# Six of eight output tiles of each down projection by one level of Strassen's scheme, with both MLPs split in two K parts

## The chip, the cores and the metric

The kernel runs on one core of a Trainium2 chip. The metric is the device time of one execution in microseconds (us). TensorE (PE) does the matmuls, ScalarE (ACT), VectorE (DVE) and GpSimd (POOL) the rest, SyncE (SP) starts the DMAs.

## The reference, cut to what matters

Three transformer layers run one after the other on 512 tokens of width 1024 (the first has 16 meta tokens besides). All is float32. The parts that the change touches are the three feed-forward blocks:

```python
def swiglu(h, w_gate, w_up, w_down):                 # first block, D_FF = 2816
    return (jax.nn.silu(h @ w_gate) * (h @ w_up)) @ w_down

def sq_relu_mlp(x, w1, w2):                          # layers 0 and 1 of the second block, D_FF_2 = 4096
    h = jax.nn.relu(x @ w1)
    return (h * h) @ w2
...
        h = rms_norm_2(x, norm_mlp_pre[layer])
        x = x + rms_norm_2(sq_relu_mlp(h, mlp_w1[layer], mlp_w2[layer]), norm_mlp_post[layer])
```

## The kernel before

Activations lie transposed: features on the 128 partitions, tokens along the columns. A projection is a set of output tiles (128 output features x 512 tokens) and each tile sums K blocks of 128 input features in one PSUM bank. Float32 accuracy comes from three fp16 matmuls for each block: high weight times high activation, high times low, low times high (L975 to L977 in `tile_T`).

**The weight stream.** All weights come as one stream of 128x128 blocks, 8 blocks (512 KB) to a unit, 317 units. SP loads each unit into `w_raw`, a ring of 6 units (`RAW`). ScalarE makes `w_hi` (fp16, scaled by `WS`) in `split_hi`, L1476; VectorE makes `w_lo`, the rest, in `split_lo`, L1878; both go into rings of 8 units (`WR`). SP loads a new unit when `lo_split` says that its place was split. ScalarE waits with `mm_done` for the matmuls that used the place it overwrites. TensorE waits for `lo_split` at a new unit.

**What sets the order.** Each engine runs a queue written out in advance; semaphores count. The class `Plan` walks over the table `STAGES` (name, kind, tiles, K, width) and numbers blocks, units, PSUM evictions (`evicted`) and banks: successive tiles take banks 0, 1, 2, 3 of `pS` in turn, in some stages also `pT` and `pO` (six in turn, `SIX`). `out_of(s, n)` on ScalarE and VectorE first runs the splits up to six units ahead, then waits until tile n's last matmul is done. So each of these two engines alternates between weight splits and evictions.

**The stages of the change.** `ffgu` (44 tiles, gate and up of the first block, K = 8 blocks) is followed by `ffd` (8 tiles, K = 22); `up0` (32 tiles, K = 8) by `dn0` (8 tiles, K = 32), and the same for `up1` and `dn1`. The first four tiles of an up stage (`lead`) are made together, block by block, while the norm before them is still arriving. VectorE evicts an up tile, squares it, ScalarE writes the high half into `ffh` and VectorE the low half.

**The end of a down projection.** For seven tiles VectorE copies the bank out (`taken`, L2517; in `ffd` it adds to X), ScalarE squares the result, and VectorE adds the squares up in `acc`. The eighth tile is computed in two token halves of 256 columns (`out_halves`, L998 to L1000, all K blocks for the first 256 tokens, then all for the others). While TensorE makes the second half, the first half's sum of squares goes through a matmul with ones (L990, L992, ahead of the second half's step 8), ScalarE takes Ln and Exp (L1536, L1538), and VectorE runs the first half of the post-norm over eight tiles (L2540, L2544). After the second half comes the same for the other tokens: the square (L1545), the eviction (L2549), the sum (L1012), Ln and Exp (L1547, L1549), and the second loop (L2561, L2567), which in layer 0 also writes the next norm's input tile by tile (L1485, L1893). The sums of squares of the two MLPs carry the names `mb` and `md`. Small matmuls on constant data (`unread`, L1130) stand between.

Of the kernel before, what the change touches and what calls it, by code (L numbers as in the profile page):

```python
# [35 lines left out]
P = 128  # L36
T = 512
# [20 lines left out]
UW = TPU * P  # L58
RAW = 6
WR = 8  # L60
# [7 lines left out]
LEADS = ("qa", "ffgu", "cv", "up0", "kvc", "up1")  # L68
SIX = ("ffgu", "cv", "up0", "up1")
SPARE = ("ks", "qb")  # L70
HOME = {"ck2": 4, "cv2": 5}
INSIDE = {"va": 0, "vb": NQ, "vm": 0, "vv": 0}


class Stage:


    def __init__(self, name, kind, n, k, width, o0, tau0):
        self.name, self.kind, self.n, self.k, self.width, self.o0, self.tau0 = name, kind, n, k, width, o0, tau0

    def tile(self, j, k):
        if self.name in LEADS and j < LEAD:
            return self.tau0 + k * LEAD + j
        return self.tau0 + (j * self.k + k if self.kind == "T" else k * self.width)


class Plan:
# [6 lines left out]
    def __init__(self):  # L94
        self.st, self.order = {}, []
        self.o = self.tau = self.ms = 0
        self.out_ms, self.unit_ms, self.out_tau, self.marks = [], {}, [], set()
        for name, kind, n, k, width in STAGES:
            while kind == "N" and self.tau % width:
                self.tau += 1  # L100
                if self.tau % TPU == 0:
                    self.unit_ms[self.tau // TPU - 1] = self.ms
# [3 lines left out]
            if kind == "T":  # L106
                if name in LEADS:
                    for kk in range(k):
                        for j in range(LEAD):
                            self.step(self.tau, 1, kk == k - 1)  # L110
                for j in range(LEAD if name in LEADS else 0, n):
                    for kk in range(k):
                        self.step(self.tau, 1, kk == k - 1)
            else:
                for t in range(n):
                    for kk in range(k):
                        tau = self.tau + kk * width
                        last = kk == k - 1
                        ends = t == n - 1 and (tau + width) % TPU == 0
# [6 lines left out]
                        if ends:  # L126
                            self.unit_ms[tau // TPU] = self.ms
                self.tau += k * width
                self.o += n
        self.n_units = -(-self.tau // TPU)  # L130
        self.bank, self.before = [], []
        turn, last = 0, {}
        for s in self.order:
            for j in range(s.n):
# [32 lines left out]
    def step(self, tau, width, last):  # L167
        ends = (tau + width) % TPU == 0
# [7 lines left out]
        if ends:  # L176
            self.unit_ms[tau // TPU] = self.ms
        self.tau += width
# [7 lines left out]
    + [("wo", "T", KD, KD, 1), ("ffgu", "T", 2 * KFF1, KD, 1), ("ffd", "T", KD, KFF1, 1),  # L186
       ("cv", "T", 12, KD, 1), ("ckv", "T", 2, KD, 1), ("kr", "T", 1, KD, 1), ("cq", "T", 6, KD, 1),
       ("kn", "T", 4, 2, 1), ("qr", "T", 2, 6, 1), ("qn", "T", 4, 6, 1), ("vm", "N", NQ, 2, 4),
       ("awo", "T", KD, KD, 1), ("up0", "T", KFF2, KD, 1), ("dn0", "T", KD, KFF2, 1),
# [3 lines left out]
       ("cwo", "T", KD, KD, 1), ("up1", "T", KFF2, KD, 1), ("dn1", "T", KD, KFF2, 1)]  # L193
# [6 lines left out]
SRC = [("mrg", 8), ("ff", KFF1), ("xb", 8), ("conv", 4), ("p1", 8), ("h0", KFF2), ("p2", 8), ("hid", 2),  # L200
       ("p3", 8), ("h1", KFF2), ("out", 16)]
# [28 lines left out]
def whole_units(name):  # L230
    return -(-PL.st[name].tau0 // TPU) * TPU
# [303 lines left out]
def splits(s, j):  # L535

    return 1 if s.name in LEADS and j < LEAD else s.k // TPU + 1
# [4 lines left out]
def build_program(nc, x_in, stream, consts, params, aux, out):  # L542
    ctx = ExitStack()
    with ctx:
# [6 lines left out]

        w_raw = sb("w_raw", [P, RAW, UW])
        w_hi = sb("w_hi", [P, WR, UW], F16)
        w_lo = sb("w_lo", [P, WR, UW], F16)
# [47 lines left out]
        ARENA = 20864  # L602
# [44 lines left out]
        ffh, at = pair(0, [KFF2, T])  # L647
        stage_c, _ = view(ARENA - KEEP_TO, [KEEP_TO])

# [25 lines left out]
        z, _ = pair(at, [5, T])  # L675
# [88 lines left out]
        raw_loaded = [sem(f"raw_loaded{i}") for i in range(RAW)]  # L764
# [67 lines left out]
        half_taken = sem("half_taken")  # L832
        lse_ln = sem("lse_ln")
# [45 lines left out]
        def m_view(m, n):  # L879

            return m_att[:, n, :] if m == "mc" else xx32[:, n, 0:T]

# [4 lines left out]
        def _(pool):  # L887
# [9 lines left out]
            norm_power("x0", meta=True)  # L897
            filled = [0]
# [21 lines left out]
            pool.wait_ge(mm_done, PL.out_ms[S["ffd"].o0 + KD - 1])  # L920
# [7 lines left out]
            pool.wait_ge(mm_done, PL.out_ms[S["dn0"].o0 + KD - 1])  # L928
# [4 lines left out]
            norm_power("p2")  # L933


        @block.tensor
        def _(pe):
            unit = [-1]

            def weights(tau, n=1):  # L940

                u = tau // TPU
# [5 lines left out]
                a = (tau % TPU) * P  # L948
                return w_hi[:, u % WR, a:a + n * P], w_lo[:, u % WR, a:a + n * P]
# [31 lines left out]
            def out_halves(s, m, rhs):  # L981

                n, q, o = HALVED.index(m), PL.q[m] + KD - 1, s.o0 + KD - 1
                bank_free(o)
                for half, ps in enumerate((pT[:, 0, 0:HT], out_bank(o)[:, HT:T])):
                    a = slice(half * HT, half * HT + HT)
                    for k in range(s.k):
# [7 lines left out]
                        tau = s.tile(KD - 1, k)  # L995
# [20 lines left out]
            def out_last(s, m, rhs):  # L1016
# [4 lines left out]
                else:  # L1021
                    out_T(s, KD - 1, rhs, inside=lambda: early_sum(m))
                    direct_norm(m)

# [330 lines left out]
            for j in range(KD - 1):  # L1355
                out_T(S["ffd"], j, of(ffh), rhs_wait=None if j else PL.r["ff"])
            out_last(S["ffd"], "x2", of(ffh))
# [101 lines left out]
        def _(act):  # L1459
# [1403 lines left out]
```

## Time and profile before

| | us |
|---|---|
| median of 3 runs | 2057.53 (2056.46 to 2060.12) |
| profiled execution, its own span | 2056.2 |
| TensorE busy | 1992.2 (97%) |
| VectorE busy | 1188.0 (58%) |
| ScalarE busy | 825.8 (40%) |
| GpSimd busy | 31.3 (2%) |

The span runs from the first to the last instruction of the profiled execution; the runs' times are 1 us longer in the median. A matmul's row shows its start and a modelled duration, and matmuls overlap, so what one costs is read from the distance between starts.

### The profile page before, as it was taken

What the parts mean: (1) busy time and instruction counts of PE and PEld (TensorE: products, weight loads), DVE (VectorE), ACT (ScalarE), POOL (GpSimd) and SP (SyncE); (2) the same over time, 40 slices, a digit from 0 to 9 for tenths busy, and PEclk for the clock granted to TensorE, in tenths of its full rate; (3) what the DMA queues carried; (4) which work ended last, traced back from release to release, by engine and by line L of the source; (5) the groups of instructions that cost most, each with busy time, mean ns of one, the idle gap of its engine ahead of it and who ended that gap; (6) DMA issues with size and microseconds to landing.
All of it is one profiled execution on the core that took longest, in us unless ns stands there. A gap on an engine that the chain in (4) does not pass through costs nothing. (4 is left out here: it accounts for less than half of the span.)

```text
span 2056.2 us, 27740 instructions
## 1 busy us (share of the span) xinstructions
PE 1992.2 (97%) x10751; PEld 965.9 (47%) x10756; DVE 1188.0 (58%) x2199; ACT 825.8 (40%) x1507; POOL 31.3 (2%) x36
## 2 busy tenths in 40 slices
PE   9989999999999999999999999999989999999998
PEld 4444444444444454444444444555544444444445
DVE  6979744546554347676575632259866636765223
ACT  4447733323333233346443322236377744432220
POOL 2000000000000002000000000000000000000000
PEclk9999999999999999999999999999999999999999
DMA  6300233324333222312233333217200031433311
GB/s 220 101 1 1 73 103 103 95 72 131 103 103 112 93 91 93 104 52 73 72 113 105 102 111 103 82 42 226 85 1 1 23 101 44 142 102 105 111 52 41
DMA packets 54345, 179.19 MB, mean 87 GB/s; under 512 B 6224, under 2 KB 11984, under 8 KB 53968
## 3 DMA queue, kind: packets, MB, share of 16 engines
q1 hardware_dynamic: 54224, 177.51, 28.0%
q8 instruction: 85, 1.39, 0.3%
q14 instruction: 36, 0.29, 0.0%
HBM read 174.34 MB, written 2.10 MB: 86 GB/s over the span
## 5 line engine op out<-in xcount | busy, mean ns | idle before, releaser
L1878 DVE SCALAR_TENSOR_TENSOR w_lo<-w_raw,w_hi 128x1024 f16<-128x1024 f32 (+1 forms) x317 | 384.4, 1217 | 178.2 <-ACT w_hi L1476 143.4
L1476 ACT ACTIVATE w_hi<-w_raw 128x1024 f16<-128x1024 f32 x316 | 330.0, 1048 | 247.8 <-PE pS L977 234.4
L975 PE MATMUL pS<-xx,w_hi 128*128 128x512 f16 x920 | 349.3, 380 | 2.4 <-DVE xx L1893 1.4
L977 PE MATMUL pS<-xx,w_lo 128*128 128x512 f16 x920 | 349.4, 380 | 0.0
L976 PE MATMUL pS<-xx,w_hi 128*128 128x512 f16 x920 | 349.2, 380 | 0.0
L975 PE MATMUL pS<-arena,w_hi 128*128 128x512 f16 x824 | 312.3, 379 | 1.4 <-DVE arena L1893 1.4
L976 PE MATMUL pS<-arena,w_hi 128*128 128x512 f16 x824 | 312.3, 379 | 0.0
L977 PE MATMUL pS<-arena,w_lo 128*128 128x512 f16 x824 | 312.3, 379 | 0.0
L1485 ACT ACTIVATE arena<-src 128x512 f16<-128x512 f32 x107 | 69.2, 647 | 322.0 <-DVE src L2581 166.7
L977 PEld LDWEIGHTS pS<-xx,w_lo 128*128 128x128 f16 x920 | 90.0, 98 | 109.0 <-issue 0.8
L975 PEld LDWEIGHTS pS<-xx,w_hi 128*128 128x128 f16 x920 | 90.2, 98 | 107.9 <-DVE xx L1893 2.2
L976 PEld LDWEIGHTS pS<-xx,w_hi 128*128 128x128 f16 x920 | 90.1, 98 | 104.0 <-issue 1.5
L975 PEld LDWEIGHTS pS<-arena,w_hi 128*128 128x128 f16 x824 | 80.7, 98 | 99.2 <-DVE arena L1893 1.9
L976 PEld LDWEIGHTS pS<-arena,w_hi 128*128 128x128 f16 x824 | 80.7, 98 | 97.5 <-issue 0.7
L977 PEld LDWEIGHTS pS<-arena,w_lo 128*128 128x128 f16 x824 | 80.7, 98 | 97.3
L1209 PE MATMUL pS<-arena 128*128 128x512 f16 (+3 forms) x480 | 103.0, 315 | 1.5 <-DVE arena L2159 1.5
L2093 DVE TENSOR_REDUCE st_max<-pT 128x1 f32<-128x512 f32 (+3 forms) x140 | 68.1, 507 | 39.3 <-PE pT L1182 32.0
L1589 ACT ACTIVATE tmp<-pS 128x512 f32<-128x512 f32 (+2 forms) x152 | 80.2, 538 | 24.5 <-PE pS L1217 16.2
L1893 DVE SCALAR_TENSOR_TENSOR arena<-src,arena 128x512 f16<-128x512 f32 x107 | 74.8, 699 | 24.9 <-ACT arena L1485 24.7
L2517 DVE TENSOR_SCALAR xx<-pS 128x512 f32<-128x512 f32 x21 | 14.5, 692 | 124.6 <-PE pS L977 124.6
L1572 ACT ACTIVATE pT<-pT,st_max 128x512 f32<-128x512 f32 (+3 forms) x140 | 72.5, 518 | 33.7 <-DVE st_max L2093 32.4
L1947 DVE TENSOR_TENSOR tmp<-pS,rs 128x512 f32<-128x512 f32 x46 | 31.7, 690 | 83.4 <-PE pS L977 83.4
(393 smaller groups left out, 2918.0 us busy)
## 6 DMA issues: line engine op xcount, KB each, us to landing
w_raw<-in_w SPq DMA_DIRECT2D x317, 512.0 KB, 3.6
X<-in_x SPq DMA_DIRECT2D x8, 264.0 KB, 6.9
arena<-in_c SPq DMA_DIRECT2D x2, 1024.0 KB, 6.1
out_t<-X SPq DMA_DIRECT2D x16, 128.0 KB, 1.7
arena<-in_h SPq DMA_DIRECT2D x4, 256.0 KB, 12.7
arena<-in_h SPq DMA_DIRECT2D x2, 512.0 KB, 9.7
arena<-in_c SPq DMA_DIRECT2D x2, 256.0 KB, 2.9
arena<-arena SPq DMA_DIRECT2D x4, 128.0 KB, 2.5
```

The source lines that it names most:

```text
L975: pe.matmul(ps, wh, ah, start=f, stop=False)
L976: pe.matmul(ps, wh, al, start=False, stop=False)
L977: mm = pe.matmul(ps, wl, ah, start=False, stop=l)
L1209: pe.matmul(ps[:, c0:c0 + n], k[:, ks_], q[:, qs], start=x == 0, stop=False)
L1476: act.activation(w_hi[:, u % WR, :], w_raw[:, u % RAW, :], ACT.Copy, scale=WS).then_inc(hi_split, 1)
L1485: act.activation(dst, a, ACT.Identity, scale=scale).then_inc(rhs_hi, 1)
L1572: ins = act.activation(a, a, ACT.Exp, bias=stat(st_max, t)[:, x:x + 1], accum_out=stat(st_sum, t)[:, x:x + 1])
L1589: act.activation(exps(u)[:, 0:a.shape[1]], a, ACT.Exp).then_inc(key_exped, 1)
L1878: dve.scalar_tensor_tensor(out=w_lo[:, u % WR, a:UW], in0=w_raw[:, u % RAW, a:UW], scalar=WS, in1=w_hi[:, u % WR, a:UW], op0=ALU.mult, op1 ...
L1893: dve.scalar_tensor_tensor(out=dst, in0=a, scalar=scale, in1=h, op0=ALU.mult, op1=ALU.subtract).then_inc(rhs_ready, 1)
L1947: dve.tensor_tensor(dst, ps, r[:, 0:T], ALU.mult).then_inc(evicted, 1)
L2093: ins = dve.tensor_reduce(stat(st_max, t)[:, x:x + 1], nat_bank(c)[:, c0:c0 + n], AX.X, ALU.max, negate=True)
```

## The change

**Strassen groups.** In each down projection tiles 1 to 6 become three groups. A group takes two output tiles, the two token halves of 256 columns, and the K blocks in pairs (even and odd), as a 2x2 by 2x2 product of blocks. Seven products replace eight: each has K/2 steps of three matmuls with 256 columns. The seven stationary operands are A11, A22 and A12 themselves and the sums S2, S3, S1, S4; the moving ones are B blocks and the combinations T1 to T4 of activations. A12 accumulates onto A11's bank, after ScalarE has copied that bank (`first_copy`, L1744). Tile 0 and tile 7 stay plain; tile 0's steps wait for the activations pair by pair (`out_pair`).

**Weight sums.** GpSimd makes four sums a group in `w_raw`, in place (`add_weights`): A21 += A11 (that is S3), then A22 becomes S2 = S3 + A22 (after A22 was split), A11 becomes S1 = S2 - A11, A12 becomes S4 = S2 + A12 (after A12 was split). There are 60 of them, 128x1024 or, in the first block, 128x1408 elements. ScalarE's splits of the sums wait for `summed`.

**K parts.** Each MLP runs as `up0a` (16 tiles), `dn0a` (all 8 output tiles, K = 16), `up0b` (16 tiles), `dn0b` (K = 16, VectorE adds to the stored result). `ffd` keeps K = 22. The two halves at the end of `dn0b` and `dn1b` have K = 16; there ScalarE's squares now wait for VectorE's evictions.

**Rings.** The three weight rings hold 66 blocks each, with units of 8, or of 11 in the first block's groups; ten load semaphores; SP's loads are written out without a loop. VectorE's and ScalarE's splits of 128x1024 become 360 in place of 318 (some are wider); hidden activations are written in pairs of tiles, with the token combinations made by VectorE (`mix_tokens`, three operations a pair).

The core of the diff:

```diff
-    + [("wo", "T", KD, KD, 1), ("ffgu", "T", 2 * KFF1, KD, 1), ("ffd", "T", KD, KFF1, 1),
+    + [("wo", "T", KD, KD, 1), ("ffgu", "T", 2 * KFF1, KD, 1), ("ffd0", "T", 1, KFF1, 1), ("ffds", "S", 3, KFF1 // 2, 1), ("ffd7", "T", 1, KFF1, 1),
...
-       ("awo", "T", KD, KD, 1), ("up0", "T", KFF2, KD, 1), ("dn0", "T", KD, KFF2, 1),
+       ("awo", "T", KD, KD, 1), ("up0a", "T", UP_A, KD, 1)] + down(0, "a") + [("up0b", "T", KFF2 - UP_A, KD, 1)] + down(0, "b")
...
+PRODUCTS = (("A11", 0, B11), ("A22", 4, T4), ("A12", 0, B21), ("S2", 1, T2), ("S3", 2, T3), ("S1", 3, T1), ("S4", 5, B22))
...
+def down(lay, part):
+
+    k = UP_A if part == "a" else KFF2 - UP_A
+    return [(f"dn{lay}{part}0", "T", 1, k, 1), (f"dn{lay}{part}s", "S", 3, k // 2, 1), (f"dn{lay}{part}7", "T", 1, k, 1)]
...
+                for g in range(s.n):
+                    s.banks.append([last.get(b, -1) for b in range(6)])
+                    o = s.o0 + N_READ * g
+                    last.update({0: o, 1: o + 1, 4: o + 2, 3: o + 3, 2: o + 4, 5: o + 5})
...
+                    pool.tensor_tensor(w["A21"], w["A11"], w["A21"], ALU.add).then_inc(summed, 1)
+                    pool.wait_ge(summed, first + 1)
+                    pool.wait_ge(lo_split, units_["A22"] + 1)
+                    pool.tensor_tensor(w["A22"], w["A21"], w["A22"], ALU.add).then_inc(summed, 1)
+                    pool.wait_ge(summed, first + 2)
+                    pool.tensor_tensor(w["A11"], w["A22"], w["A11"], ALU.subtract).then_inc(summed, 1)
+                    pool.wait_ge(lo_split, units_["A12"] + 1)
+                    pool.tensor_tensor(w["A12"], w["A22"], w["A12"], ALU.add).then_inc(summed, 1)
...
+            def strassen(s, g, ops, copies):
+
+                free = s.banks[g]
+                for x, (name, b, op) in enumerate(PRODUCTS):
+                    if name == "A12":
+                        pe.wait_ge(first_copied, copies + g + 1)
+                    elif free[b] >= 0:
+                        pe.wait_ge(evicted, free[b] + 1)
...
+                    for k in range(s.k):
+                        tau = s.factor(g, x, k)
+                        wh, wl = weights(tau)
+                        oh, ol = ops[0][:, k, a], ops[1][:, k, a]
+                        pe.matmul(ps, wh, oh, start=k == 0 and name != "A12", stop=False, skip_group_check=True)
...
+            def first_copy(s, g, copies, f):
+
+                ms, tau = s.first_ms[g]
+                split_hi(tau, look=0)
+                act.wait_ge(evicted, s.o0 + (N_READ * (g - 1) + 2 if g else 0))
+                act.wait_ge(mm_done, ms)
+                act.activation(x1c, pS[:, 0, 0:HT], ACT.Copy, scale=f).then_inc(first_copied, 1)
...
+            def mix_tokens():
...
+                link(dve.tensor_tensor(in_two(sums[:, 0:T]), in_two(b[:, HT:3 * HT]), twice(b[:, 3 * HT:4 * HT]), ALU.subtract))
...
-                if m == "x2":
+                if m in ("x2", "mb", "md"):
                     act.wait_ge(evicted, o + 1)
...
             sp.wait_ge(mm_done, PL.out_ms[S["kvc"].o0 - 1])
+            sp.wait_ge(rhs_ready, PL.r["p2"] + KD)
```

VectorE's queue at the start of layer 0's down projection stood like this before (`xx` holds the result, `acc` the squares):

```order
L1878 SCALAR_TENSOR_TENSOR w_lo<-w_raw,w_hi 128x1024 [waits hi_split] x4
L2517 TENSOR_SCALAR xx<-pS 128x512 [waits mm_done]
L1900 COPY acc<-sq 128x512 [waits squared]
L1878 SCALAR_TENSOR_TENSOR w_lo<-w_raw,w_hi 128x1024 [waits hi_split] x4
L2517 TENSOR_SCALAR xx<-pS 128x512 [waits mm_done]
L1903 TENSOR_TENSOR acc<-acc,sq 128x512 [waits sq_summed,squared]
```

Now, at the start of part a, tile 0 and the first group stand there like this (`arena` holds the result, `tmp` the intermediate combinations):

```order
L2753 TENSOR_SCALAR arena<-pS 128x512 [waits mm_done]
L2180 SCALAR_TENSOR_TENSOR w_lo<-w_raw,w_hi 128x1024 [waits hi_split] x2
L2753 TENSOR_SCALAR arena<-pS 128x256 [waits mm_done]
L2180 SCALAR_TENSOR_TENSOR w_lo<-w_raw,w_hi 128x1024 [waits hi_split] x2
L2764 SCALAR_TENSOR_TENSOR tmp<-pS,tmp 128x256 [waits first_copied,mm_done]
L2766 SCALAR_TENSOR_TENSOR tmp<-pT,tmp 128x256 [waits evicted]
L2180 SCALAR_TENSOR_TENSOR w_lo<-w_raw,w_hi 128x1024 [waits hi_split] x2
L2768 SCALAR_TENSOR_TENSOR tmp<-pS,tmp 128x256 [waits mm_done]
L2774 SCALAR_TENSOR_TENSOR arena<-pS,tmp 128x512 [waits evicted]
L2180 SCALAR_TENSOR_TENSOR w_lo<-w_raw,w_hi 128x1024 [waits hi_split]
L2780 SCALAR_TENSOR_TENSOR arena<-pO,tmp 128x256 [waits mm_done]
```

One eviction for every four splits has become six evictions for every seven splits.

ScalarE's queue in the same place, before (high halves of units, and the squares of evicted tiles):

```order
L1476 ACTIVATE w_hi<-w_raw 128x1024 [waits mm_done,raw_loaded0]
L1497 ACTIVATE sq<-xx 128x512 [waits sq_summed,evicted]
L1476 ACTIVATE w_hi<-w_raw 128x1024 [waits mm_done,raw_loaded1]
L1476 ACTIVATE w_hi<-w_raw 128x1024 [waits mm_done,raw_loaded2]
L1476 ACTIVATE w_hi<-w_raw 128x1024 [waits mm_done,raw_loaded3]
```

Now, from the copy of one group's first product to that of the next:

```order
L1744 ACTIVATE tmp<-pS 128x256 [waits mm_done,evicted]
L1735 ACTIVATE w_hi<-w_raw 128x1024 [waits raw_loaded2,mm_done]
L1735 ACTIVATE w_hi<-w_raw 128x1024 [waits raw_loaded1,mm_done]
L1735 ACTIVATE w_hi<-w_raw 128x1024 [waits raw_loaded3,mm_done]
L1735 ACTIVATE w_hi<-w_raw 128x1024 [waits summed,mm_done] x4
L1744 ACTIVATE tmp<-pS 128x256 [waits mm_done,evicted]
```

Four splits a group wait for GpSimd's sums, and they stand ahead of the next copy.

VectorE's queue at the end of layer 0's last down projection, from the end of the first half's loop to the second loop, before:

```order
L2544 TENSOR_TENSOR X<-X,tmp 128x256 [waits dve_chain] x2
L1878 SCALAR_TENSOR_TENSOR w_lo<-w_raw,w_hi 128x1024 [waits hi_split] x4
L2549 TENSOR_SCALAR xx<-pS 128x256 [waits squared,mm_done]
L2561 SCALAR_TENSOR_TENSOR tmp<-xx,par,rs 128x256 [waits dve_chain,rs_direct,half_taken]
L2567 TENSOR_TENSOR X<-X,tmp 128x256 [waits dve_chain]
```

And now:

```order
L2921 TENSOR_TENSOR X<-X,tmp 128x256 [waits dve_chain] x2
L2180 SCALAR_TENSOR_TENSOR w_lo<-w_raw,w_hi 128x1024 [waits hi_split] x2
L2752 SCALAR_TENSOR_TENSOR arena<-pS,arena 128x256 [waits mm_done]
L2936 SCALAR_TENSOR_TENSOR tmp<-arena,par,rs 128x256 [waits dve_chain,rs_direct,half_taken]
L2942 TENSOR_TENSOR X<-X,tmp 128x256 [waits dve_chain]
```

Two splits have left this place, and the eviction no longer waits for ScalarE's square.

## Rows read from the trace of the kernel before

**Rows 1.** The head of the page, busy time, share of the span, instructions.

```profile
span 2056.2 us, 27740 instructions
PE 1992.2 (97%) x10751; PEld 965.9 (47%) x10756; DVE 1188.0 (58%) x2199; ACT 825.8 (40%) x1507; POOL 31.3 (2%) x36
```

**Rows 2.** Table by stretches: length, busy time by engine, PEclk, DMA share, GB/s.

```profile
667.00:753.60 86.60, 86.60 (x436) 42.48 (x434) 26.01 (x28) 20.57 (x22) 0.00 (x0) 1.00 0.27 84
...
1183.00:1338.00 155.00, 155.00 (x768) 74.88 (x767) 46.24 (x50) 35.16 (x37) 0.00 (x0) 1.00 0.31 97
...
1355.10:1359.10 4.00, 3.99 (x11) 1.49 (x12) 3.21 (x7) 2.73 (x5) 0.00 (x0) 0.57 0.62 239
```

**Rows 3.** Lines by form, 1183 to 1338: busy, mean ns | idle before, releaser.

```profile
L1878 DVE SCALAR_TENSOR_TENSOR w_lo<-w_raw,w_hi 128x1024 f16<-128x1024 f32 x28 | 34.2, 1223 | 61.6 <-ACT w_hi L1476 61.6
L1903 DVE TENSOR_TENSOR acc<-acc,sq 128x512 f32<-128x512 f32 x6 | 4.1, 683 | 0.1
...
L1476 ACT ACTIVATE w_hi<-w_raw 128x1024 f16<-128x1024 f32 x28 | 29.6, 1056 | 92.7 <-PE pS L977 92.7
```

**Rows 4.** Timeline, TensorE in `ffd`: start, duration, instruction.

```profile
739.82 0.38 PE L975 MATMUL pS<-arena,w_hi 128*128 128x512 f16 x1
...
746.08 0.38 PE L977 MATMUL pS<-arena,w_lo 128*128 128x512 f16 x1
746.29 0.27 PE L998 MATMUL pT<-arena,w_hi 128*128 128x256 f16 x1
...
751.32 0.27 PE L999 MATMUL pT<-arena,w_hi 128*128 128x256 f16 x1
```

**Rows 5.** Timeline at the end of tile 6 of `dn1`.

```profile
2022.23 0.38 PE L977 MATMUL pS<-arena,w_lo 128*128 128x512 f16 x1
...
2022.45 0.27 PE L998 MATMUL pT<-arena,w_hi 128*128 128x256 f16 x1
...
2022.65 0.69 DVE L2517 TENSOR_SCALAR xx<-pS 128x512 f32<-128x512 f32 x1 [17.16 <-PE pS L977]
...
2023.26 0.68 DVE L1903 TENSOR_TENSOR acc<-acc,sq 128x512 f32<-128x512 f32 x1
```

**Rows 6.** Timeline of the tail of `dn1`, from the second half on.

```profile
2032.93 0.27 PE L998 MATMUL pS<-arena,w_hi 128*128 128x256 f16 x1
...
2037.58 0.88 DVE L2540 SCALAR_TENSOR_TENSOR tmp<-xx,par,rs 128x256 f32<-128x256 f32 x2 [3.54 <-ACT rs L1538]
...
2042.76 0.76 DVE L2544 TENSOR_TENSOR X<-X,tmp 128x256 f32<-128x256 f32 x2
...
2044.91 0.38 ACT L1545 ACTIVATE sq<-pS 128x256 f32<-128x256 f32 x1 [7.37 <-PE pS L1000]
2046.08 0.47 ACT L1547 ACTIVATE rs<-pO,eps 128x256 f32<-128x256 f32 x1 [0.79 <-PE pO L1012]
2046.59 0.42 ACT L1549 ACTIVATE rs<-rs 128x256 f32<-128x256 f32 x1
...
2047.10 0.48 DVE L2561 SCALAR_TENSOR_TENSOR tmp<-xx,par,rs 128x256 f32<-128x256 f32 x1 [1.27 <-ACT rs L1549]
```

**Rows 7.** Timeline of the tail of `dn0`.

```profile
1337.99 0.27 PE L998 MATMUL pS<-arena,w_hi 128*128 128x256 f16 x1
...
1348.49 4.62 DVE L1878 SCALAR_TENSOR_TENSOR w_lo<-w_raw,w_hi 128x1024 f16<-128x1024 f32 x4
1353.04 0.41 DVE L2549 TENSOR_SCALAR xx<-pS 128x256 f32<-128x256 f32 x1
1353.37 0.47 DVE L2561 SCALAR_TENSOR_TENSOR tmp<-xx,par,rs 128x256 f32<-128x256 f32 x1
...
1355.11 0.40 PE L1081 MATMUL pS<-xx,w_hi 128*128 128x512 f16 x1 [2.06 <-ACT xx L1485]
```

**Rows 8.** GpSimd's lines by form: busy, mean ns of one.

```profile
L895 POOL TENSOR_TENSOR rt<-rt,half_neg 128x4 f32<-128x4 f32 x4 | 4.1, 1014 | 469.0 <-DVE rt L1912 469.0
...
L902 POOL MEMSET arena<- 128x768 f32 x1 | 0.7, 738 | 0.1
...
L902 POOL MEMSET arena<- 128x512 f32 x1 | 0.5, 526 | 0.1
```

More of the change, by code:

```diff
@@ L105, in __init__ @@
             self.order.append(s)
-            if kind == "T":
+            if kind == "S":
+                for g in range(n):
+                    self.group(s, g)
+            elif kind == "T":
                 if name in LEADS:
@@ L118, in __init__ @@
                         last = kk == k - 1
-                        ends = t == n - 1 and (tau + width) % TPU == 0
+                        ends = t == n - 1 and full[kk]
                         if last or ends:
@@ L165, in __init__, with tile, group, step @@
             at += n
-    def step(self, tau, width, last):
-        ends = (tau + width) % TPU == 0
+    def tile(self):
+        if not self.open:
+            self.raw.append(len(self.raw_size))
+            self.freed.append(len(self.size))
+            self.size.append(0)
+            self.raw_size.append(0)
+            self.open = True
+        self.unit.append(len(self.size) - 1)
+        self.off.append(self.size[-1])
+        self.size[-1] += 1
+        self.raw_size[-1] += 1
+        self.open = self.size[-1] < TPU
+    def group(self, s, g):
+        raw = {name: len(self.raw_size) + n for n, name in enumerate(RAWS)}
+        v = {name: len(self.size) + n for n, (name, _, _) in enumerate(PRODUCTS)}
+        self.raw_size += [s.k] * len(RAWS)
+        self.freed += [v[FREED_BY[name]] for name in RAWS]
+        self.sums[v["S2"]] = (raw, v, self.n_sums)
+        self.n_sums += 4
+        ends = []
+        for name, _, _ in PRODUCTS:
+            self.size.append(s.k)
+            self.raw.append(raw[HELD_IN[name]])
+            self.unit += [v[name]] * s.k
+            self.off += range(s.k)
+            self.tau += s.k
+            self.ms += 1
+            self.marks.add((self.tau - 1, 0))
+            self.unit_ms[v[name]] = self.ms
+            ends.append((self.ms, self.tau - 1))
+        s.first_ms.append(ends[0])
+        for x in (2, 3, 3, 5, 5, 6):
+            self.out_ms.append(ends[x][0])
+            self.out_tau.append(ends[x][1])
+        self.o += N_READ
+    def step(self, tau, last):
+        self.tile()
+        ends = not self.open
         if last or ends:
@@ L176, in step, with reach @@
         if ends:
-            self.unit_ms[tau // TPU] = self.ms
-        self.tau += width
+            self.unit_ms[self.unit[tau]] = self.ms
+        self.tau += 1
+    def reach(self, tau, look, stop):
+        now = self.unit[tau]
+        v = now + 1
+        while v < min(now + 1 + look, stop) and self.after[v] <= now - 2:
+            v += 1
+        return v
+def down(lay, part):
+    k = UP_A if part == "a" else KFF2 - UP_A
+    return [(f"dn{lay}{part}0", "T", 1, k, 1), (f"dn{lay}{part}s", "S", 3, k // 2, 1), (f"dn{lay}{part}7", "T", 1, k, 1)]
 STAGES = (
@@ L230, in whole_units, with unit_at, raw_at @@
 def whole_units(name):
-    return -(-PL.st[name].tau0 // TPU) * TPU
+    t = PL.st[name].tau0
+    return PL.unit[t] + (PL.off[t] > 0)
+def unit_at(name):
+    return PL.unit[PL.st[name].tau0]
+def raw_at(name):
+    return PL.raw[unit_at(name)]
 CAUSAL_NAT = (((3, 0, 0, 4 * P),), ((2, 0, 0, 3 * P), (0, 3 * P, 0, P)), ((1, 0, 0, 2 * P),))
```

578 lines of the change are left out of this document (407 added, 171 removed).

## The prediction

> **What bounds the kernel now.** I read the head of the page first: TensorE is busy 1992.2 of 2056.2 us, VectorE 58% of it [rows 1]. That is an average, so I took the table by stretches next: in the plain run of the down projections TensorE has no gap at all (86.60 of 86.60 us in the first block's, 155.00 of 155.00 in layer 0's), while VectorE works 26.01 and 46.24 us there [rows 2]. The same stretch's list of lines says what VectorE does: 28 splits of a weight unit into its low half at 1.223 us, whose idle time is ended by ScalarE's high half [rows 3], and that one waits for TensorE to give back ring places. So in these stages a matmul removed is time removed, provided the other engines follow. Around them are places where TensorE does wait: the tails of the down projections, where a norm runs (term 3).
>
> The profiled execution spans 2056.2 us; the median of the runs is 2057.53. I make the sum on the span and add 1.3.
>
> **Term 1, the matmuls.** Over one step of K a tile costs three matmuls of 512 columns. Between the starts at 739.82 and 746.08 lie 29 of them: 0.2159 us each. Half-width ones run from 746.29 to 751.32 in 46 steps: 0.1093 us each, so the weight load does not show at 256 columns either [rows 4]. A group of two plain tiles costs 2K x 3 x 0.2159 = 1.295K; as Strassen products it is 7 x K/2 x 3 x 0.1093 = 1.148K. Three groups save 0.443K. K is 22 in the first block and 32 in each MLP (two parts of 16): 0.443 x 86 = 38.1 us off. The other tiles and the up projections keep their matmuls.
>
> **Term 2, banks handed over at once.** Before, consecutive tiles lie in different banks, so an eviction costs TensorE nothing. Now tile 0 of each MLP part, the first product after it, tile 7 of part a and the first tile of the second up half all use bank 0 of pS. At three places a layer (tile 0 to A11 in both parts, tile 7 to the up half) TensorE must wait for the eviction of what it has just finished. The end of a tile of before prices it: the last matmul starts at 2022.23, the next could at 2022.45; VectorE starts its eviction at 2022.65, takes 0.69, and its next operation starts at 2023.26 [rows 5]. TensorE would go on at about 2023.3, 0.85 us late. Six places cost 5.1 us. In layer 0's part b VectorE lays a bias first and has splits ahead of that eviction: up to 0.9 more. I take 6.0 (bounds 3, were banks handed over at the operation's first columns, and 10, were a 1.2 us split ahead at half the places and more).
>
> **Term 3, the tails of the two MLPs.** Before, the last tile's second half holds 32 steps, 32 x 3 x 0.1093 = 10.5 us, and beside it the first half's norm runs on VectorE. Now it holds 16, 5.25 us; term 1 counted this as if the end came 5.25 us earlier, since the rest of part b's K was moved ahead of the second up half. But the norm's loop is as long as before. In layer 1 the second half starts at 2032.93, VectorE's loop runs from 2037.58 to 2043.52 (t+4.65 to t+10.6), the square follows at 2044.91 and the second loop begins at 2047.10, t+14.2 [rows 6]. After: the sums of the norm stand at the same step (k = 8), so the loop ends at t+10.6 again. Then come the eviction (0.47), ScalarE's square, which now waits for that eviction (0.4), the matmul with ones (0.7), Ln and Exp (0.9): with hand-overs the second loop begins at about t+13.3. It gains 0.9 of the 5.2, so 4.3 us are lost. In layer 0 the loop ends at t+10.5 (1348.49 less 1337.99), four splits ran before the eviction, and the second loop began at t+15.4 [rows 7]. Now two splits stand there (2.4 us): eviction at 12.9, square, sum, Ln, Exp: t+15.5. Nothing is gained and 5.3 lost. TensorE is then idle some 6 to 7 us in each tail; after a 2.06 us wait before 1355.11 the stretch behind it shows a granted clock of 0.57 [rows 2, 7], so the small matmuls after the longer gap may run at the lower level: 1 us. Term 3 is +10.6 (9 to 13).
>
> **Term 4, do the other engines follow?** A group's seven products last 7 x 24 x 0.1093 = 18.4 us in an MLP part and 25.2 in the first block. VectorE does seven splits (8.5 us at 1.22; in the first block 1408 columns wide, about 1.6 each by the step from 512 to 1024 columns) and six evictions of some 3 us: 11.5 in part a, 14 in part b with the additions to the old value and the squares, 16.7 in the first block. ScalarE: seven halves at 1.05, a copy, two squares, 9 us. Both fit.
>
> GpSimd is the unknown: 60 additions of two weight blocks, no such row in the trace. From below: VectorE handles 1024 columns of two operands in 1.22 us. From above: a GpSimd memset of 512 columns takes 526 ns, of 768 738, about 1 ns a column with one access each [rows 8]; three accesses of 1.03 would be 3.2 us. In between, the fixed part of its 128x4 operation (1.014) plus one pass over 1024 columns is 2.1; I take it, as the trace's only two-input GpSimd operation shows that start. Four sums are then 8.4 us of 18.4, 9.8 of 25.2 in the first block. *The Trainium skill, "GPSIMD Engine Reference", section 3.1, gives 4497 ns for an add of 2048 columns; halved, an estimate of 2.25 us a sum, it would move the total by under 1 us. No trace row bears on it.*
>
> Latency: ScalarE's split of a sum waits for GpSimd, and behind it in ScalarE's queue stands the copy of the next group's first product, for which the third product waits. In an MLP part the unit rings let the sums run about half a group ahead; in the first block, where a block takes 11 of the ring's 66 places, raw loads wait for splits of the group in flight and I find 2 us of room (a group's raw blocks are 44 of 66, so half the next group's loads wait for this group's splits of S3 and S4). I put +4 for this, nearest to the case of sums at 2.1 us (0 with sums at VectorE's price; the upper end is rival B).
>
> The up halves: a pair of tiles lasts 48 x 0.2159 = 10.4 us; VectorE does two evictions, the token sums, two wide low halves and two splits, 1.4 + 1.5 + 2.4 + 2.4 = 7.7. The last pair is ready some 5.7 us after tile 0 begins, and tile 0 takes it last. Cost nothing while VectorE keeps 2 us of room a pair. On SP an added wait for the second norm of layer 1 stands ahead of the compressed bias; behind it are queued the weight loads from the stage q2b on, which the ring would not take earlier anyway, since 16 units of other stages lie before them: nothing.
>
> **Sum:** 2056.2 - 38.1 + 6.0 + 10.6 + 4 = 2038.7 span, 2040 us.
>
> **Rivals.**
>
> A, the smaller losses: the sums never show and hand-overs cost 3: 2056.2 - 38.1 + 3 + 9 + 1.3 = 2031. For it: VectorE and ScalarE have 40% of a group free.
>
> B, **slower**: VectorE and GpSimd do not run side by side. Place: the groups. If VectorE's operations on two SBUF operands (splits, additions, squares) and GpSimd's sums take turns, a group needs at 3.2 us a sum 8.5 + 12.8 = 21.3 us in part a, 11 + 12.8 = 23.8 in part b (2.5 more for the additions and two squares at 0.683 [rows 3]) and 13.7 + 17.6 = 31.3 in the first block: 2.9 x 6 + 5.4 x 6 + 6.1 x 3 = 68 us over TensorE's time. Tiles 0 give each of five stages some 8 us of lead, 40 in all at best, so 28 to 68: with 45 in place of the 4 the time is 2081. It decides from 26 us in all, 1.7 a group, with the lead a sum of 2.6 to 3. Against it: no row shows VectorE slowed beside GpSimd, which works only 31.3 us in all [rows 1], nearly all of it memsets. *The Trainium skill, "SBUF — State Buffer", section "SBUF: two separate sides", states this: a VectorE instruction with two SBUF inputs and a GpSimd instruction that reads SBUF hold a shared port pair in turn, whichever starts first. No row here shows it or denies it.*
>
> C, turns at the middle price: at 2.4 us a sum, part b lacks 11 + 9.6 - 18.4 = 2.2 a group and VectorE's blocked queue delays evictions too; about +17 instead of +4: 2053.
>
> D, the change does less than it says: the products at 256 columns cost more than 0.1093, because their stationary blocks change at every matmul. There are 3 x 43 x 21 = 2709 of them; at 0.114 they give back 12.7 us: 2053. Against it, the 46 even steps in rows 4, with a new weight load each.
>
> **How the numbers follow.** Forecast 0.50 (2034 to 2050), A 0.15, B 0.15, C 0.15, D 0.05. About 0.2% (4 us) is what a measurement here can tell from no change. Forecast and A are faster; C and D straddle 2053.4, half each: faster 0.75, same 0.09, slower 0.16. The range reaches from 2030 to 2062 and leaves out most of B and a little of A.
>
> **What would show it.** TensorE's start-to-start in the products at 0.109; gaps of some 0.85 us at the first product of each part and at the first tile of the second up half; second norm loops starting t+13.3 and t+15.5; GpSimd's sums near 2.1 us; the wait before the third product (A12) on ScalarE's copy under 1 us. Wrong would be: sums of 3 us, or VectorE's splits stretched well over 1.22 us beside them, or waits of TensorE for low splits inside the groups.

## The result, and the profile after

The changed kernel takes 2096.52 us (2092.26 to 2097.2), the one before 2057.21 in the same comparison: a ratio of 1.0187 (95% interval 1.0174 to 1.0200). It is slower; the forecast was 2040, with 2062 as the upper end. The profiled execution spans 2090.4 us; it was the fastest of the four, 4.3 us under the median. The head of its page answers to [rows 1]:

```profile
span 2090.4 us, 29726 instructions
PE 1970.2 (94%) x11816; PEld 1074.7 (51%) x11821; DVE 1435.5 (69%) x2400; ACT 949.0 (45%) x1628; POOL 212.0 (10%) x96
```

TensorE's busy time fell by 22 us, yet it now waits 120 us instead of 64. Which waits these are, the list of TensorE's waits says (line waited for, then us in total, times, longest):

```profile
PE pS L1239 <- ACT tmp L1744: 18.6, 6, 6.1
PE pO L1212 <- ACT sq L1835: 13.2, 3, 6.3
PE pS L1239 <- issue: 11.3, 4, 5.1
...
PE pS L1331 <- DVE w_lo L2180: 6.7, 1, 6.7
PE pS L1269 <- DVE arena L2195: 6.5, 4, 3.3
...
PE pS L1173 <- DVE arena L2753: 1.6, 2, 0.8
```

L1239 is the first matmul line of a Strassen product, L1744 ScalarE's copy of a group's first product, L1269 tile 0 of a part. The third line ("issue": nothing that the profile shows released it) is the first product of each MLP part, which waits for tile 0's bank. L1173 is here the first tile of the second up half, which waits for tile 7's bank. L1212 stands in the tails. The wait at L1331 lies at the very start of the program, where the change was not expected to do anything.

The table by stretches answers to [rows 2]: the groups of the first block, of part b in layer 0 and in layer 1, then the wait for one first copy and what follows it (length, busy by engine, granted clock, DMA share, GB/s):

```profile
670.58:758.95 88.37, 79.44 (x694) 69.42 (x693) 63.76 (x48) 30.17 (x29) 30.38 (x9) 0.94 0.33 117
1299.50:1362.91 63.41, 58.58 (x504) 50.79 (x505) 43.62 (x47) 24.98 (x29) 20.98 (x7) 0.94 0.40 140
2000.66:2062.39 61.73, 56.92 (x504) 49.88 (x505) 40.06 (x43) 19.81 (x24) 20.99 (x7) 0.97 0.15 51
705.60:709.20 3.60, 0.00 (x0) 0.00 (x0) 3.60 (x2) 1.27 (x4) 2.36 (x1) 0.57 0.00 0
709.20:712.80 3.60, 3.56 (x17) 2.55 (x18) 2.20 (x2) 2.51 (x2) 0.00 (x0) 0.50 0.52 153
```

Three groups should last 75.7 us in the first block and 55.0 in a part; they take 88.4, 63.4 and 61.7. After this wait TensorE restarts at a granted clock of 0.50, the lower of its two levels, 1.2 GHz: 17 matmuls in 3.6 us where 33 fit.

From the starts of the products and tiles in the trace the whole difference comes together (us; a gain is negative):

| place | forecast | measured |
|---|---|---|
| matmuls of the products | -38.1 | -38.1 (2.62 and 3.60 us a product) |
| start of the program | 0 | +9.8 |
| tile 0 of the four MLP parts, until the first product | +4.3 | +20.8 |
| tile 7 of part a to the up half | +1.7 | +1.9 |
| waits for the first copy, six | +4 | +19.6 |
| lower clock level inside the groups | 0 | +11.4 |
| tails of the three down projections | +10.6 | +12.8 |
| other stages, between the blocks | 0 | -4.0 |
| span | -17.5 | +34.2 |

Tile 0, for instance, starts at 1115.84 and the first product at 1132.44: 16.6 us where 48 matmuls of 0.2159 last 10.4.

```profile
1115.84 0.38 PE L1269 MATMUL pS<-arena,w_hi 128*128 128x512 f16 x1
...
1132.44 0.37 PE L1239 MATMUL pS<-arena,w_hi 128*128 128x256 f16 x1 [2.19 <-issue]
```

The place of the last row is the attention of layer 1, and the row belongs to this one execution, not to the change. From its first plain tile (1406.74) to that of the next up half (1757.43) it takes 350.7 us here, 354.0 in the kernel before, and 354.8 in the run with the start mended, whose code in that place is the changed kernel's. In the middle of it (1485 to 1600) the granted clock is 0.99 here and 0.96 in that run.

**What VectorE does beside a sum.** The trace's timeline in the first block, GpSimd and VectorE together (start, duration):

```profile
693.92 0.41 DVE L2768 SCALAR_TENSOR_TENSOR tmp<-pS,tmp 128x256 f32<-128x256 f32 x1
694.14 3.16 POOL L1085 TENSOR_TENSOR w_raw<-w_raw 128x1408 f32<-128x1408 f32 x1 [3.16 <-DVE w_lo L2180]
694.37 3.48 DVE L2771 TENSOR_TENSOR X<-X,tmp 128x512 f32<-128x512 f32 x1
697.38 3.50 POOL L1087 TENSOR_TENSOR w_raw<-w_raw 128x1408 f32<-128x1408 f32 x1
697.77 3.39 DVE L2772 TENSOR_TENSOR X<-X,tmp 128x256 f32<-128x256 f32 x1
701.19 0.69 DVE L2774 SCALAR_TENSOR_TENSOR X<-pS,X 128x512 f32<-128x512 f32 x1
...
703.50 4.47 POOL L1089 TENSOR_TENSOR w_raw<-w_raw 128x1408 f32<-128x1408 f32 x1 [2.62 <-DVE w_lo L2180]
...
704.87 0.41 DVE L2752 SCALAR_TENSOR_TENSOR X<-pO,X 128x256 f32<-128x256 f32 x1
705.20 3.04 DVE L2202 COPY acc<-sq 128x512 f32<-128x512 f32 x1
705.32 0.63 ACT L1790 ACTIVATE sq<-X 128x512 f32<-128x512 f32 x1 [5.28 <-DVE X L2752]
708.28 0.63 ACT L1790 ACTIVATE sq<-X 128x512 f32<-128x512 f32 x1 [2.33 <-DVE acc L2202]
708.82 0.37 ACT L1744 ACTIVATE tmp<-pS 128x256 f32<-128x256 f32 x1
709.24 0.40 PE L1239 MATMUL pS<-arena,w_hi 128*128 128x256 f16 x1 [6.07 <-ACT tmp L1744]
```

An addition of 512 columns takes 3.48 us and one of 256 columns 3.39: they end 0.55 and 0.28 us after a sum ends, and the same forms take 0.69 and 0.42 where GpSimd is idle. The evictions that read one operand from PSUM do not wait: L2752 takes 0.41 in the middle of a sum. But the additions ahead of it were late, so the group's last eviction (L2752) comes only at 704.87. ScalarE's two squares of this group wait for it; the second waits 2.33 us more for the copy L2202, which ends at 708.24, behind the sum that started at 703.50. Behind the squares in the queue stands the copy of the next group's first product, for which TensorE waits 6.1 us.

### The profile page after: what moved, and what is told of

Read it like the earlier page. It is cut to its first block and busy times, and to the rows that moved or that the text cites. A ratio compares the mean times of both kernels' runs of the same rounds, so it can differ in the third digit from the quotient of the medians.

```text
span 2090.4 us, 29726 instructions
## 1 busy us (share of the span) xinstructions
PE 1970.2 (94%) x11816; PEld 1074.7 (51%) x11821; DVE 1435.5 (69%) x2400; ACT 949.0 (45%) x1628; POOL 212.0 (10%) x96
## 5 line engine op out<-in xcount | busy, mean ns | idle before, releaser
L2180 DVE SCALAR_TENSOR_TENSOR w_lo<-w_raw,w_hi 128x1024 f16<-128x1024 f32 (+3 forms) x359 | 485.4, 1363 | 101.3 <-ACT w_hi L1735 65.8
L1735 ACT ACTIVATE w_hi<-w_raw 128x1024 f16<-128x1024 f32 (+1 forms) x358 | 375.1, 1063 | 213.3 <-POOL w_raw L1085 63.6
L1173 PE MATMUL pS<-xx,w_hi 128*128 128x512 f16 x952 | 361.3, 380 | 6.6 <-DVE w_lo L2180 3.6
L1239 PE MATMUL pS<-arena,w_hi 128*128 128x256 f16 x645 | 181.3, 281 | 29.9 <-ACT tmp L1744 18.6
L1240 PE MATMUL pS<-arena,w_hi 128*128 128x256 f16 x645 | 181.2, 281 | 0.0
L1241 PE MATMUL pS<-arena,w_lo 128*128 128x256 f16 x645 | 181.0, 281 | 0.0
L1173 PEld LDWEIGHTS pS<-xx,w_hi 128*128 128x128 f16 x952 | 93.2, 98 | 116.4 <-issue 4.8
L1082 POOL TENSOR_TENSOR w_raw<-w_raw 128x1024 f32<-128x1024 f32 (+1 forms) x15 | 44.1, 2938 | 928.5 <-DMA w_raw<-in_w 928.5
L1778 ACT ACTIVATE arena<-src 128x1024 f16<-128x1024 f32 (+1 forms) x64 | 60.5, 945 | 113.8 <-DVE src L2743 47.3
L1778 ACT ACTIVATE arena<-sq 128x1024 f16<-128x1024 f32 x43 | 45.5, 1057 | 117.8 <-DVE sq L2722 117.8
L1173 PE MATMUL pS<-arena,w_hi 128*128 128x512 f16 x254 | 96.3, 379 | 1.5 <-DVE arena L2195 1.5
L1174 PE MATMUL pS<-arena,w_hi 128*128 128x512 f16 x254 | 96.3, 379 | 0.0
L1175 PE MATMUL pS<-arena,w_lo 128*128 128x512 f16 x254 | 96.3, 379 | 0.0
L1239 PEld LDWEIGHTS pS<-arena,w_hi 128*128 128x128 f16 x645 | 65.0, 101 | 43.3 <-ACT tmp L1744 20.2
```

The source lines that it names most:

```text
L1173: pe.matmul(ps, wh, ah, start=f, stop=False)
L1174: pe.matmul(ps, wh, al, start=False, stop=False)
L1175: mm = pe.matmul(ps, wl, ah, start=False, stop=l)
L1239: pe.matmul(ps, wh, oh, start=k == 0 and name != "A12", stop=False, skip_group_check=True)
L1240: pe.matmul(ps, wh, ol, start=False, stop=False, skip_group_check=True)
L1241: mm = pe.matmul(ps, wl, oh, start=False, stop=k == s.k - 1, skip_group_check=True)
```

## The experiments

Two causes are to be told apart, and the start is a third matter. *Turns*: VectorE's operations on two SBUF operands and GpSimd's sums run one at a time. *Order*: what stands ahead of what in ScalarE's queue and which bank follows which would cost the same whoever makes the sums.

**The start.** Up to the split at 11.29 ScalarE's order is that of before. Then the timeline of the changed kernel reads:

```profile
11.29 1.04 ACT L1735 ACTIVATE w_hi<-w_raw 128x1024 f16<-128x1024 f32 x1
...
18.03 0.63 ACT L1790 ACTIVATE sq<-X 128x528 f32<-128x528 f32 x1
18.56 3.88 ACT L1735 ACTIVATE w_hi<-w_raw 128x1024 f16<-128x1024 f32 x4
```

Four units are split behind all the input copies; before, the third was split at 13.79, between two of them. The planner's look-ahead asks that a ring place's last reader lies two units back, and for a place never used it finds -1, which at unit 0 is not.

```diff
-        while v < min(now + 1 + look, stop) and self.after[v] <= now - 2:
+        while v < min(now + 1 + look, stop) and (self.after[v] < 0 or self.after[v] <= now - 2):
```

> One condition in the planner's look-ahead: a ring place that was never used counts as free, so the weight splits of the first projection stand between the input copies again, as before the change. Theory: the first plain tiles start 10.3 us later after the change (40.77 against 30.50 us) because four high-half splits stand behind all eight input copies in ScalarE's queue; with the condition mended the time falls by about 10 us, to 2086 to 2088. Rival: the start is late because the loads from the new stream layout land later (10.5 us median in the first 60 us against 8.4); then the time falls by less than 2 us.

2086.39 us: 10.1 less, and the first plain tile starts at 30.98. The layout of the loads is not the cause.

**Sums on 8 columns.**

```diff
-                    pool.tensor_tensor(w["A21"], w["A11"], w["A21"], ALU.add).then_inc(summed, 1)
+                    pool.tensor_tensor(w["A21"][:, 0:8], w["A11"][:, 0:8], w["A21"][:, 0:8], ALU.add).then_inc(summed, 1)
```

(and the three others alike)

> GpSimd's 60 sums work on 8 columns in place of 1024 or 1408, so the weights of four of seven products are not the sums; all waits and their order stay. Theory (turns): sums of 2.4 to 3.2 us block VectorE's operations on two SBUF operands; without them the six waits for the first copy (19.5 us), the late last pairs and evictions at tile 0 (some 16 us) and the half-clock stretches behind these stalls (some 11 us) go: about 2050. Rival (queue order): the copy of the first product is late because two squares stand ahead of it on ScalarE and wait for the last eviction of the group before; then at least half of the 19.5 us stays: 2062 or more.

2049.17 us, 47.4 less, and no first copy is waited for any more. The queue order alone costs little, then, as long as VectorE is on time. This run takes away both what a sum blocks and the time until it is ready; the next one tells the two apart.

**Fills in place of the sums.**

```diff
-                    pool.tensor_tensor(w["A21"], w["A11"], w["A21"], ALU.add).then_inc(summed, 1)
+                    pool.memset(w["A21"].bitcast(F16), 0.5).then_inc(summed, 1)
```

(and the three others alike)

> Each of GpSimd's sums is replaced by a fill of the same block that only writes (2048 or 2816 fp16 columns of a constant, about 1.9 and 2.6 us by the fill rows of before), so the products use constants in place of sums; order and waits stay. Theory (turns): a GpSimd instruction that reads nothing from SBUF does not block VectorE, its 128x512 additions fall from 2.6 to 3.5 back to 0.69 us, and the time is within 6 us of the kernel with short sums, about 2052. Rival (latency of the sums alone, no blocking): ScalarE and TensorE wait for GpSimd as before, 2085 or more.

2047.07 us, although GpSimd is busy 145.9 us here: a fill of a block of 1024 lasts 1.80 us (a sum that nothing delays 2.35) and is waited for like a sum. So not the time until a sum is ready costs the 47 us but what the sum blocks on VectorE; a fill, which reads nothing from SBUF, does not block the additions. VectorE's lines by form show it (count | busy, mean ns). The changed kernel:

```profile
L2722 DVE TENSOR_TENSOR sq<-src,sq 128x256 f32<-128x256 f32 x43 | 28.5, 663 | 1.5
L2202 DVE COPY acc<-sq 128x512 f32<-128x512 f32 x12 | 7.7, 638 | 1.5 <-ACT sq L1790 1.5
L2772 DVE TENSOR_TENSOR X<-X,tmp 128x256 f32<-128x256 f32 x3 | 7.2, 2397 | 0.0
```

With fills:

```profile
L2722 DVE TENSOR_TENSOR sq<-src,sq 128x256 f32<-128x256 f32 x43 | 18.3, 425 | 1.5
L2202 DVE COPY acc<-sq 128x512 f32<-128x512 f32 x12 | 6.4, 534 | 1.5 <-ACT sq L1790 1.5
L2772 DVE TENSOR_TENSOR X<-X,tmp 128x256 f32<-128x256 f32 x3 | 1.3, 418 | 0.0
```

The additions fall to their free time. The Trainium skill, "SBUF — State Buffer", section "SBUF: two separate sides", states just this lock, between a VectorE instruction with two SBUF inputs and a GpSimd instruction that reads SBUF; the trace agrees: 2397 ns beside sums, 418 beside fills. The copy L2202 is held up by both. Its mean hides one slow row in twelve: the 3.04 us shown above beside a sum, and here 1.79 us beside a fill, to 0.28 us after its end.

```profile
696.55 2.44 POOL L1089 MEMSET w_raw<- 128x2816 f16 x1
...
697.48 1.79 DVE L2202 COPY acc<-sq 128x512 f32<-128x512 f32 x1
```

**The squares behind the next first copy.**

```diff
                 for g in range(s.n):
                     first_copy(s, g, copies, f)
+                    if m is not None and g:
+                        squares(g - 1)
                     for x in (0, 1, 3, 5):
                         out_of(s, N_READ * g + x)
-                    if m is not None:
-                        act.wait_ge(evicted, s.o0 + N_READ * g + N_READ)
-                        for n in (2 * g + 1, 2 * g + 2):
-                            square(PL.q[m] + n, out_to(m, n))
```

> Only ScalarE's order: the two squares of a Strassen group stand behind the copy of the next group's first product, not ahead of it. Theory (queue order): the first product of the next group waits for VectorE's last eviction of the group before only through these squares; the six waits (19.5 us) go, and with them three of the half-clock stretches (some 6 us): about 2071. Rival (turns alone): the copy stays late because the splits of GpSimd's sums stand ahead of it as well: less than 5 us is gained.

2074.95 us, 21.6 less, 4 short of the expected gain. Of the six waits for the first copy one is left, in the first block:

```profile
PE pS L1239 <- ACT tmp L1744: 2.2, 1, 2.2
```

Both are needed, then: turns make VectorE late, and this order hands its lateness to TensorE.

**Start, squares and banks together.**

```diff
-HOME = {"ck2": 4, "cv2": 5}
+HOME = {"ck2": 4, "cv2": 5, "dn0a0": 2, "dn0b0": 2, "dn1a0": 2, "dn1b0": 2, "dn0a7": 1, "dn1a7": 1}
```

(with the two edits above)

> Three edits of order together: the start mended (10.1 us alone), the squares behind the next first copy (21.6 us alone), and tile 0 of each MLP part in bank 2 and tile 7 of part a in bank 1, so that no matmul needs a bank that was just finished. Theory (turns): the sums still block VectorE around the last pair of each up half, but its late eviction no longer stops TensorE: 2096.5 - 10.1 - 21.6 - 1.9 (tile 7) - 7 to 10 (the waits of 5.1, 2.7, 2.2 and 1.3 us at the first products and part of the half-clock stretch behind them) = 2053 to 2056. Rival: these waits are for the pairs' low halves and splits, not for the bank, and stay: 2063.

2046.75 us, below the kernel before (0.9944, 0.9927 to 0.9961), and 6 to 9 better than expected: 49.8 less in all, of which 31.7 are the two edits' own, so the banks brought 18.1, if they add. That is about the waits at the first products (11.3), the lower clock level behind three of them (1.3 to 1.8 each, of which I had counted little) and tile 7 (1.9). GpSimd still makes the sums here. The table by stretches, groups of the first block and of both parts b:

```profile
660.59:741.70 81.11, 76.30 (x695) 67.50 (x693) 63.05 (x48) 29.96 (x29) 29.62 (x9) 1.00 0.33 113
1273.43:1329.39 55.96, 55.20 (x506) 49.25 (x505) 46.88 (x53) 27.25 (x32) 20.98 (x7) 1.00 0.40 139
1963.34:2018.36 55.02, 55.02 (x506) 49.31 (x505) 42.61 (x46) 21.59 (x26) 21.01 (x7) 1.00 0.18 59
```

Parts b last 56.0 and 55.0 us, so VectorE keeps pace there in spite of the turns. Only the first block's groups still lose to them, 5.5 us.

**Sums held until the last pair.**

```diff
+                if name.startswith("dn"):
+                    pool.wait_ge(rhs_ready, PL.r["h" + name[2]] + (UP_A if name[3] == "a" else KFF2))
```

(and the splits of these sums barred until tile 0's last unit)

> The same as the run with start, squares and banks, and GpSimd begins the sums of an MLP part's first group only when the part's last pair is ready; ScalarE's and VectorE's splits of these sums then stand behind tile 0. Theory (turns): the waits for the last pairs at tile 0 (3.3 and 2.7 us measured in parts a) go, and the sums lie beside tile 0's splits: 4 to 8 us under that run. Rival: the first sum (S2) now comes too late for the fourth product, TensorE waits there 2 us or more in each of four parts and nothing is gained.

2071.71 us, 25 worse. The pairs came on time (tile 0 lasts its 10.4 us in all four parts), but neither theory had this: TensorE now waits 5.8 to 6.7 us for the copy of the first group in each of the four parts. The fifth wait, 2.4 us in the first block, was there before.

```profile
PE pS L1246 <- ACT tmp L1751: 27.2, 5, 6.7
...
1108.61 8.91 DVE L2193 SCALAR_TENSOR_TENSOR w_lo<-w_raw,w_hi 128x1024 f16<-128x1024 f32 x3 [6.04 <-ACT w_hi L1742]
...
1118.15 0.38 ACT L1751 ACTIVATE tmp<-pS 128x256 f32<-128x256 f32 x1 [7.13 <-DVE arena L2766]
```

In the timeline of part a ScalarE's first copy starts at 1118.15, after it has waited 7.1 us for tile 0's eviction; that stands on VectorE behind the low splits of three units, which took 8.9 us in turns with GpSimd, where three free ones take 3.7.

**Strassen undone alone.** Tiles 1 to 6 are plain tiles, without sums.

```diff
-    return [(f"dn{lay}{part}0", "T", 1, k, 1), (f"dn{lay}{part}s", "S", 3, k // 2, 1), (f"dn{lay}{part}7", "T", 1, k, 1)]
+    return [(f"dn{lay}{part}0", "T", 1, k, 1), (f"dn{lay}{part}s", "T", KD - 2, k, 1), (f"dn{lay}{part}7", "T", 1, k, 1)]
```

> Strassen undone alone: tiles 1 to 6 of each down projection are plain tiles again, without sums, first copies and half-width products; the K parts, the pairs of activations with their token combinations, the rings and the late start stay. Theory: time before plus the start (10.1) plus the two shortened tails (10.6 by the forecast's own working): 2078, within 4. Rival: the K parts cost nothing by themselves and the tails belong to Strassen's longer queue on VectorE: 2067.

2075.20 us, within what was expected: 17.8 over the kernel before (2057.42 in this comparison), of which the start is 10.1; the 7.7 left are the K parts with their tails and whatever else stays, taken together. Strassen's products with their sums made the kernel 21.3 us slower (2096.5 against 2075.2), where 38.1 were to be gained.

**The sums on VectorE.** With start, squares and banks as above.

```diff
-            add_weights("dn0as")
...
+                    if v + 2 in PL.sums:
...
+                        dve.tensor_tensor(w["A21"], w["A11"], w["A21"], ALU.add).then_inc(summed, 1)
+                        dve.wait_ge(summed, first + 1)
+                        dve.tensor_tensor(w["A22"], w["A21"], w["A22"], ALU.add).then_inc(summed, 1)
+                        dve.wait_ge(summed, first + 2)
+                        dve.tensor_tensor(w["A11"], w["A22"], w["A11"], ALU.subtract).then_inc(summed, 1)
...
+                        dve.tensor_tensor(w["A12"], w["A22"], w["A12"], ALU.add).then_inc(summed, 1)
```

> The same as the run with start, squares and banks, but VectorE makes the 60 sums itself, three behind the low split of A22 and one behind that of A12; GpSimd does none. By the trace of before 1024 columns cost it 1.2 us, so a group costs 16.4 us of its time in part a, 18.9 in part b (TensorE's group lasts 18.4) and 23.1 of 25.2 in the first block. Theory (turns): 4.8 us of VectorE's own time a group costs less than being blocked for GpSimd's 9.6: 2042 to 2048, under both kernels. Rival: VectorE is the bound in part b and, with three sums in a row ahead of an eviction, makes TensorE wait about 2 us a group: 2060 or more.

2033.96 us: 0.9883 of the time before (0.9866 to 0.9899), the fastest of all, and 8 us under the range that I expected. A sum of 1024 columns takes VectorE 1.225 us. The table by stretches, groups of the first block and of both parts b:

```profile
660.93:736.58 75.65, 75.65 (x694) 67.81 (x693) 56.76 (x56) 30.19 (x29) 0.00 (x0) 1.00 0.38 133
1261.58:1316.60 55.02, 55.02 (x506) 49.31 (x505) 48.12 (x59) 26.73 (x31) 0.00 (x0) 1.00 0.46 162
1949.95:2004.97 55.02, 55.02 (x506) 49.31 (x505) 42.22 (x53) 19.89 (x24) 0.00 (x0) 1.00 0.17 58
```

TensorE has no gap in any group, at full clock (those of both parts a last 55.02 us too), with VectorE busy 87% of layer 0's part b and 77% of layer 1's. Tile 0 of each part now lasts its 10.4 us: no pair is late and no bank is waited for.

**The sums on VectorE, nothing else.** The changed kernel with that edit alone.

> The changed kernel with one edit: VectorE makes the 60 sums, GpSimd none; start, squares and banks as the change has them. Theory (turns): with nothing reading SBUF on GpSimd, the evictions come on time, so the squares ahead of the first copy cost nothing, as with the short sums (2049.2); VectorE's own 60 sums of 1.2 to 1.6 us add 77 us of work, of which what shows is near the first products: 2050 to 2056, and against the best run (2034.0) the start accounts for 10.1 and the banks for 4 to 6. Rival (order alone): the squares and banks are what costs, whoever makes the sums: 2034.0 + 10.1 + 21.6 + 4 = 2070.

2060.56 us, between the two theories and above what I expected: 36.0 of the 47.4 us go, while 5.3 us of waits for the first copy and 6.9 for banks stay:

```profile
PE pS L1234 <- issue: 6.9, 4, 3.1
PE pS L1234 <- ACT tmp L1739: 5.3, 5, 2.7
```

VectorE's own sums delay its evictions a little: in layer 0's part b it works without a pause from 1290.17 to 1304.54, four sums among the work, and evicts the first group's last product, for which the squares wait, at 1304.12, 3.8 us after that product's last matmul started. From here to the fastest kernel the start, squares and banks bring 26.6.

## Why the prediction was wrong

**Term 1 held.** A product of 8 blocks takes 2.62 us, one of 11 blocks 3.60, as 24 and 33 times 0.1093, where the granted clock is full.

**Term 2** was sized for an eviction that is on time. Tile 7 to the up half came out at 0.95 us, against 0.85. At tile 0 the four places cost 20.8 in place of 4.3, but 4.2 in the run with the short sums, so the hand-over was priced rightly and the eviction was late. The first group's sums run while VectorE makes the token sums of the last pairs, whose three operations took 2.23, 2.45 and 2.45 us, start to end, in layer 0 (0.68, 0.42 and 0.42 where no sum runs):

```profile
1111.90 3.21 POOL L1087 TENSOR_TENSOR w_raw<-w_raw 128x1024 f32<-128x1024 f32 x1
...
1113.43 2.23 DVE L2717 TENSOR_TENSOR sq<-src 128x512 f32<-128x512 f32 x1
...
1115.08 2.79 POOL L1089 TENSOR_TENSOR w_raw<-w_raw 128x1024 f32<-128x1024 f32 x1
...
1115.70 2.45 DVE L2719 TENSOR_TENSOR sq<-src,sq 128x256 f32<-128x256 f32 x1
...
1117.83 2.53 POOL L1082 TENSOR_TENSOR w_raw<-w_raw 128x1024 f32<-128x1024 f32 x1
...
1118.19 2.45 DVE L2722 TENSOR_TENSOR sq<-src,sq 128x256 f32<-128x256 f32 x1
```

I gave the up halves 2 us of room a pair and did not ask what GpSimd does there.

**Term 3 held.** In layer 1 the second half starts at 2067.64 and the second loop at 2081.32, t+13.7 (forecast t+13.3); in layer 0 it is t+16.0 (1368.15 to 1384.12; forecast t+15.5). The losses are 4.8 and 6.0, 10.8 together, against the forecast 10.6; the first block's tail, which the sum left out, took 2.0 more.

**Term 4 failed, in its frame more than in its price.** I set 4 us for the sums and gave the turns 0.30, as rivals B and C; the waits for the first copy alone came to 19.6, and the short sums gave back 47.4.

The price came out near by luck: a sum of 1024 columns that nothing delays lasts 2.35 us, where I took 2.1. The Trainium skill's figure, halved, was an estimate of 2.25 ("GPSIMD Engine Reference", section 3.1). I had taken 1.014 us of start from an operation on four columns that raises to a power. An addition of 8 columns takes 0.20 us (short sums), and from 1024 to 1408 columns a sum grows from 2.35 to 3.16, 2.1 ns a column, twice the one pass that I added. Beside VectorE the 48 sums of 1024 columns took 2.88 in the mean.

Rivals B and C asked whether a group's turns add up to more than TensorE's 18.4 us, and let them cost only what lies above it. At 2.35 a sum, part a would fit and part b would lack 2 us a group. But with only start, squares and banks mended and the sums still on GpSimd, parts b last 56.0 and 55.0 us of 55.0: not the sum of the turns decided there. What decided is where a blocked operation stands: ahead of an eviction, ahead of the last pair, and, through the squares in ScalarE's queue, ahead of the first copy. In parts a, where ScalarE has no squares, no first copy was waited for in the changed kernel either. I counted those two squares as 1.3 us of ScalarE's time and overlooked that they wait for the group's last eviction, with the copy queued behind them. That is the rule that I applied to the splits of the sums and not to the squares.

**Not in the sum at all** were the start (9.8 us), where ScalarE's queue had been changed by a rule of the planner, outside the stages that the change speaks of, and the clock: seven of the ten waits at first products and first copies are followed by 2.6 to 3.6 us at the lower level, 11.4 us lost in all. I allowed 1 us for it, in the tails only.

With the short sums (47.4) and the start (10.1) taken off, 2096.5 becomes 2039.0, if they add (no run has just these two). The forecast without its 4 us for the sums was 2036. So what it left out is in the main these two and what follows from them.

## What to carry to other kernels

Before work is given to an idle engine, ask what it shares with the busy one: here GpSimd's 60 two-operand sums were cheaper on VectorE itself (78 us of its time, with no gap of TensorE in the groups) than beside it. Read the lateness, not the load: for each instruction that the main engine waits for, list what stands ahead of it in its queue and what each of those waits for. And go over the order of every engine from the first row, since a planner's rule that is changed for one stage acts in all.

## What the runs showed of the hardware

An operation of VectorE with two SBUF operands that meets a running GpSimd sum waits for all of it (3.4 us for 0.42 of work), while one that reads one operand from PSUM keeps its time (0.41 to 0.69). GpSimd is held up too: sums of 1408 columns last 3.16 us alone and up to 4.47 beside VectorE. Beside fills, which only write, the two-operand operations keep their times (0.42, 0.69). Unexpected was the float32 copy L2202, with one SBUF input: it waited out a sum (3.04 us) and also a fill (1.79), and takes 0.42 otherwise. That is one row in each run. And a wait of TensorE can cost more than itself: 29.9 us of waits at first copies and first products drew 11.4 us behind them, in matmuls at 1.2 GHz.
